# The second of every two gathered expert rows summed on VectorE instead of TensorE, in the PEER stage of a decoder layer

## The reference, cut to what matters

```python
g = jax.nn.softmax(best_s, axis=-1)
a = jax.nn.gelu(jnp.einsum('nd,nhkd->nhk', hx, expert_u[eidx])) * g      # 128 numbers per token
return jnp.einsum('nhk,nhkd->nd', a, expert_v[eidx])                      # weighted sum of 128 rows of V
```

## Time and profile before

| | us |
|---|---|
| median of 3 runs (lowest, highest) | 4863.4 (4863.33, 4865.5) |
| the profiled execution | 4853.14 |
| its span, first to last instruction | 4851.3 |
| busy in it: TensorE, VectorE, ScalarE, GpSimd | 3906.1, 2540.8, 1380.6, 1277.3 |

### The profile page before, as it was taken

One profiled execution on the slowest core, in us unless ns is written; L12 is line 12 of the kernel. 1 busy time (PEld: TensorE's weight loads), 2 busy tenths in 40 slices (PEclk: granted clock), 3 DMA queues, 4 the chain that ended last, 5 costly groups with the idle time before them and its releaser, 6 DMA issues.

```text
span 4851.3 us, 41498 instructions
## 1 busy us (share of the span) xinstructions
PE 3906.1 (81%) x13477; PEld 2361.7 (49%) x13477; DVE 2540.8 (52%) x6112; ACT 1380.6 (28%) x4112; POOL 1277.3 (26%) x1078
## 2 busy tenths in 40 slices
PE   6788979999963999777998987777768777777786
PEld 5457366888853888643444442323223323232232
DVE  1564543433534112275867866557557465575574
ACT  1355432322321111212332332323223223222232
POOL 0000000001000000004444544444444445445443
PEclk8889979995985899888999999999999999999999
DMA  3000111303014111229999999999999999999998
GB/s 140 5 2 12 39 49 33 98 36 122 36 62 156 52 40 67 109 69 378 403 421 410 412 419 414 420 421 411 421 420 411 421 417 418 422 412 422 420 411 355
DMA packets 219012, 1235.30 MB, mean 255 GB/s; under 512 B 25226, under 2 KB 51242, under 8 KB 85426
## 3 DMA queue, kind: packets, MB, share of 16 engines
q0 software_dynamic: 154512, 1117.85, 56.0%
q1 hardware_dynamic: 62834, 112.83, 6.8%
q10 hardware_dynamic: 1456, 2.04, 0.1%
HBM read 1210.15 MB, written 22.48 MB: 254 GB/s over the span
## 4 chain that ended last, share of the span: by engine, by line
DMA 29%; PE 16%; DVE 8%; ACT 2%; POOL 2%; issue 2%; POOLq 0%; SPq 0%; DVEq 0%; ACTq 0%
DMA ff_rows<-in_uv,pk_expert 28%; PE banks L2018 12%; DVE ff_rows L1827 3%; PE banks L1981 2%; POOL ff_rows L1790 2%; ACT ff_diag L1898 1%; PE banks L1991 1%; DVE pk_cand L1646 1%; DVE pk_cand L1643 1%; DVE pk_axes L1648 1%; ACT ff_a L1891 1%; ACT ff_gelu L1886 0%; PE banks L1944 0%; DMA ff_rows<-in_uv,ff_pick_tail 0%; DVE topi L1738 0%
## 5 line engine op out<-in xcount | busy, mean ns | idle before, releaser
L2018 PE MATMUL banks<-ff_rows,ff_diag 128*128 128x512 f32 x4128 | 1940.7, 617 | 577.5 <-ACT ff_diag L1898 562.4
L1790 POOL DMA_INDIRECT ff_rows<-in_uv,pk_expert x1024 | 1234.1, 1205 | 2075.3 <-PE banks L2018 1208.4
L1827 DVE CUSTOM_DVE_ANT_0 ff_rows<-ff_rows,ff_h_row 128x1024 f32<-128x1024 f32 x1032 | 1251.7, 1224 | 970.5 <-DMA ff_rows<-in_uv,pk_expert 957.9
L2018 PEld LDWEIGHTS banks<-ff_rows,ff_diag 128*128 128x128 f32 x4128 | 770.3, 194 | 1686.7 <-ACT ff_diag L1898 843.0
L1886 ACT ACTIVATE ff_gelu<-ff_dots 128x2 f32<-128x2 f32 x516 | 104.9, 203 | 1802.2 <-DVE ff_dots L1827 1801.9
L1898 ACT ACTIVATE ff_diag<-ident,ff_a 128x128 f32<-128x128 f32 x1024 | 355.0, 394 | 16.7
L173 PE MATMUL banks<-d_w_high,h_high 128*128 128x512 f32 (+1 forms) x648 | 274.2, 423 | 33.9 <-DVE d_w_low L180 33.6
L174 PE MATMUL banks<-d_w_low,h_high 128*128 128x512 f32 (+1 forms) x648 | 264.7, 408 | 0.0
L175 PE MATMUL banks<-d_w_high,h_low 128*128 128x512 f32 (+1 forms) x648 | 263.9, 407 | 0.0
L1891 ACT ACTIVATE ff_a<-ff_gelu,pk_gate 128x1 f32<-128x1 f32 x1024 | 245.7, 287 | 16.8
L1073 POOL DMA_DIRECT2D d_w<-in_w_dil x7 | 4.0, 575 | 884.9 <-POOLq L120 695.7
(11 more groups left out here) (343 smaller groups left out, 4704.6 us busy)
## 6 DMA issues: line engine op xcount, KB each, us to landing
d_w<-in_w_dil POOLq DMA_DIRECT2D x9, 2048.0 KB, 8.5
d_w<-in_w_ada POOLq DMA_DIRECT2D x32, 512.0 KB, 4.6
ff_w<-in_w_pq SPq DMA_DIRECT2D x32, 512.0 KB, 4.5
ff_rows<-in_uv,pk_expert POOLq DMA_INDIRECT x1024, 15.7
w_ada<-in_w_ada SPq DMA_DIRECT2D x16, 512.0 KB, 3.5
ds_kv<-in_state SPq DMA_DIRECT2D x8, 1024.0 KB, 8.1
mx_w<-in_w_gate SPq DMA_DIRECT2D x16, 512.0 KB, 5.6
o_group<-da_o SPq DMA_DIRECT2D x24, 260.0 KB
```

What stands on the lines that cost most here:

```text
L1790: pool.indirect_dma_start(out=rows[r][:, :], out_offset=None, in_=IN["uv"][:, :], in_offset=bass.IndirectOffsetOnAxis(ap=at, axis=0))\
L1827: ins = dve.tensor_tensor_reduce(rows[r][:, 0:D], rows[r][:, 0:D], h_row[t % 2][:], 1.0, 0.0, ALU.mult, ALU.add, dots[:, B % RB, j:j + 1])
L2018: ins = pe.matmul(A[0:n, half, :], diag[:, B % DB, j, 0:n], rows[r][:, D + half * 512:D + (half + 1) * 512], **ends)
```

## The change

In each batch the first pick is summed as before, by products on TensorE. The second is summed on VectorE by one scaled addition, acc = v * a + acc, over 128 x 1024 numbers in SBUF. The first batch of a tile sets acc by a scaled copy. There are two accumulators, taken in turn by tiles. `diag` holds one matrix for a batch instead of two. VectorE does the addition of batch B - 1 after the two dots of batch B (and ahead of whatever picking is placed there). GpSimd now waits for the addition too (`vsum`), before it reuses the buffers. At the end of a tile `turn_out` waits for the additions, and makes each 128 x 128 block of T by two products into the same bank: `out` by the identity, and `acc` by the identity (for the sample tile by `ownerT`, which also sums the 16 partitions of a token).

```diff
-        diag = sb("diag", [P, DB, G, P])
+        diag = sb("diag", [P, DB, P])
+        acc = [sb(f"acc{i}", [P, D]) for i in range(2)]
@@ GpSimd, before the gathers of batch B
                     if B >= RB:
                         pool.wait_ge(s["sum"], B - RB + 1)
+                        pool.wait_ge(s["vsum"], B - RB + 1)
@@ VectorE
+                def sums(B):
+                    t, b = batches[B]
+                    r = B % RB * G + 1
+                    v, weight = rows[r][:, D:2 * D], a[:, B % RB, 1:2]
+                    dve.wait_ge(s["a"], B + 1)
+                    if b == 0:
+                        if t >= 2:
+                            dve.wait_ge(s["turn"], t - 1)
+                        ins = dve.tensor_scalar(acc[t % 2][:], v, weight, None, ALU.mult)
+                    else:
+                        dve.wait_ge(s["vsum"], B)
+                        ins = dve.scalar_tensor_tensor(out=acc[t % 2][:], in0=v, scalar=weight, in1=acc[t % 2][:], op0=ALU.mult,
+                                                       op1=ALU.add)
+                    ins.then_inc(s["vsum"], 1)
...
                     ins.then_inc(s["dot"], 1)
+                    if B:
+                        sums(B - 1)
...
+                sums(len(batches) - 1)
                 add_out(LAST - 1)
@@ ScalarE
-                    for j in range(G):
-                        ins = act.activation(diag[:, B % DB, j, 0:width], base[:, 0:width], ACT.Copy,
-                                             scale=a[:, B % RB, j:j + 1])
-                    ins.then_inc(s["diag"], 1)
+                    act.activation(diag[:, B % DB, 0:width], base[:, 0:width], ACT.Copy, scale=a[:, B % RB, 0:1])\
+                       .then_inc(s["diag"], 1)
@@ TensorE, turn_out
+                    pe.wait_ge(s["vsum"], first[t + 1])
+                    turned = c.ident if t < LAST else ownerT
                     for m in range(KD):
-                        ins = pe.transpose(T[:, m // 4, (m % 4) * P:(m % 4) * P + n], out[0:n, m * P:(m + 1) * P],
-                                           c.ident[0:n, 0:n])
+                        at = T[:, m // 4, (m % 4) * P:(m % 4) * P + n]
+                        pe.matmul(at, out[0:n, m * P:(m + 1) * P], c.ident[0:n, 0:n], start=True, stop=False)
+                        ins = pe.matmul(at, acc[t % 2][:, m * P:(m + 1) * P], turned[:, 0:n], start=False, stop=True)
@@ TensorE, batch loop
-                    for j in range(G):
-                        r = B % RB * G + j
-                        ends = dict(start=(b == 0 and j == 0), stop=(B + 1 == first[t + 1] and j == G - 1))
-                        for half in range(2):
-                            ins = pe.matmul(A[0:n, half, :], diag[:, B % DB, j, 0:n],
-                                            rows[r][:, D + half * 512:D + (half + 1) * 512], **ends)
+                    r = B % RB * G
+                    for half in range(2):
+                        ins = pe.matmul(A[0:n, half, :], diag[:, B % DB, 0:n],
+                                        rows[r][:, D + half * 512:D + (half + 1) * 512], start=(b == 0),
+                                        stop=(B + 1 == first[t + 1]))
```

More of the change, by code:

```diff
@@ L1718, in stage_ffn @@
         s = {n: c.sem("ff_" + n) for n in ("keys_in q_mm q_copy sc_mm sc_copy top small_in x_in stored tail_out tail_in "
-                                           "ht htc h_mm h_copy dot gelu a diag sum out turn y").split()}
+                                           "ht htc h_mm h_copy dot gelu a diag sum vsum out turn y").split()}
         Q, S, A, T = c.psum[:, 0:2], c.psum[:, 2:4], c.psum[:, 4:6], c.psum[:, 6:8]
```

## The result

The changed kernel takes 4965.23 us (median of 3 runs, 4963.03 to 4968.35) where the kernel before takes 4863.4: a ratio of 1.0218, with a 95% interval of 1.0197 to 1.0239. It is 102 us slower; the forecast was 81 slower, 4944 in a range of 4880 to 5005. The profiled execution is the median run, with a span of 4963.4 us against 4851.3.

The account below looks back on a forecast made before the run. The prediction took the gathers in `stage_ffn` to bound the kernel at 421 GB/s. Its terms, 48 (six tiles) + 32 (first two) + 1 (end), gave +81 us on 4863.4: 4944 us, range 4880 to 5005.

Parts of the forecast that it names:

- The bound, and TensorE's relief: In `stage_ffn`, gathers bind at 421 GB/s; halving TensorE's products to 1.85 us a batch is worth nothing in undisturbed batches.
- The addition: VectorE's scaled addition of 128x1024, once a batch: 1.29 us, or 1.21 us with overlap, bounds 1.15 and 1.35.
- The delay, and the cover: Picking stretch, tiles three to eight: batch 32's release 16.2 us late, queue covers 6.5, loss 10.4 a tile; +48 us.
- the better case among its unknown costs: Gather queue able to shrink to the shortest landing seen, 5.6 us: 2.9 us less in each of eight tiles, -23.
- The 0.7 that the prediction had to add: Fifth tile before the change: the delay rule gave 2.7 us lost, the window 3.4; the difference was added to each loss.
- The first two tiles: `top16` also on VectorE there: release of batch 32 27.2 us late, 21.4 us lost a tile, +16 each, +32 us.
- The end: After the last batch, `turn_out` issues 16 products for 8 transposes, twice: +1 us (0 to +3).
- Backlog: VectorE's late work round the picking delays buffer release and gathers: +48 us for six tiles, +32 for the first two.
- Issue bound: Rival: with VectorE full, GpSimd's gather issue binds; 2.75 us a gather loses 7 us a tile, +58, 5002 us; chance 0.10.
- Clock: Rival: TensorE falls to 1.2 GHz, costing time in the first two tiles; 5069 us throughout, 4991 for half; chance 0.07.
- Double rate: Rival: the addition runs as fast as the scaled copy, cost 0.67 us; +23, 4887 us, or no change, 4864; chance 0.09.
- Faster: Rival: present losses come from TensorE, so halved products win up to 25 us; three quarters give 4845 us; chance 0.06.

Follow-up runs that it names:

- e1_relief: Changed kernel without the scaled additions on VectorE, the gathers' wait for them and the second product of each turn; 4846.4 us, 0.9968 of the kernel before.
- e6_half_add: Changed kernel with VectorE waits behind each `top16` part and `differences`, and the addition over 512 of 1024 columns; 4879.3 us, 1.0037 of the kernel before.
- e5_two_waits: Changed kernel with VectorE waiting for its own last instruction behind each `top16` part and behind `differences`; 4924.0 us, 1.0135 of the kernel before.
- e2_both: Changed kernel with the second pick's products made on TensorE as well, beside the additions (two diagonals, four products a batch); 4943.6 us, 1.0184 of the kernel before.
- e4_wait: Changed kernel with VectorE waiting for its own last instruction behind each `top16` part only; 4933.5 us, 1.0152 of the kernel before.
- e9_dot_wait: Changed kernel with VectorE waiting for the batch's own two dots ahead of each addition; 4940.5 us, 1.0185 of the kernel before.
- e3_order: Changed kernel with the six tiles of each `top16` part in reverse order, the 8-partition instruction first; 4944.7 us, 1.0181 of the kernel before.

## Why the prediction was right, and where it was off

**The bound, and TensorE's relief.** Right. The undisturbed window stays at 422 GB/s with VectorE 73.5% busy (forecast 421 and 71%), and the relief alone is worth 2.5 us of stage (e1_relief).

**The addition.** Right: 1280 ns in the median, forecast 1.29 us. In the row of 3777.66 to 3781.15 of the fifth tile dots and additions follow each other as the forecast had them:

```profile
3777.66 1.22 DVE L1844 CUSTOM_DVE_ANT_0 ff_rows<-ff_rows,ff_h_row 128x1024 f32<-128x1024 f32 x1
...
3778.81 1.28 DVE L1834 SCALAR_TENSOR_TENSOR ff_acc<-ff_rows,ff_a,ff_acc 128x1024 f32<-128x1024 f32 x1
3780.01 1.22 DVE L1844 CUSTOM_DVE_ANT_0 ff_rows<-ff_rows,ff_h_row 128x1024 f32<-128x1024 f32 x1
3781.15 1.22 DVE L1844 CUSTOM_DVE_ANT_0 ff_rows<-ff_rows,ff_h_row 128x1024 f32<-128x1024 f32 x1
```

The addition takes 3780.01 - 3778.81 = 1.20 us net; the forecast took 1.21.

**The delay, and the cover.** The delay was right, the cover was too small. GpSimd's timeline of the changed kernel in the fifth tile, the gathers of batch 20 and of batch 37 (which reuses the buffers of 32):

```profile
3679.43 1.48 POOL L1792 DMA_INDIRECT ff_rows<-in_uv,pk_expert  x1 [2.57 <-DVE ff_acc L1834]
...
3780.86 1.17 POOL L1792 DMA_INDIRECT ff_rows<-in_uv,pk_expert  x1 [8.60 <-DVE ff_acc L1834]
```

They are 101.4 us apart, undisturbed it would be 17 x 4.97 = 84.5: 16.9 us late, forecast 16.2. The tile lost 8.4, so the queue covered 8.5 of them. Its landings say the same: 14.2 us in an undisturbed window, down to 5.7 in this tile's picking stretch.

```profile
DMA to landing us min/median/max: 14.2/14.2/15.1
...
DMA to landing us min/median/max: 5.7/11.0/16.7
```

The prediction had 5.8 (15.0 - 8.5 - 0.7). It had named the better case among its unknown costs, a queue that shrinks to 5.6 us, worth 23 us less; this is what happened, with 5.7. Why did the sum not have it? It measured the old kernel's worst delay from batch 25. But batch 25 was late itself. Batch 20 of that tile was issued here:

```profile
3603.88 0.94 POOL L1790 DMA_INDIRECT ff_rows<-in_uv,pk_expert  x1 [3.11 <-PE banks L2018]
```

From it to batch 38 at 3705.03 it is 101.15 - 18 x 4.97 = 11.7 us late, and not 9.9 (which should read 10.0, as 74.60 - 64.6); with 3.6 lost, 8.1 were covered. Counted from batch 20 the four kernels agree: before 11.7 late, 3.6 lost; e6_half_add 10.9 and 3.8; changed 16.9 and 8.4; e5_two_waits 17.9 and 9.2. The cover is 7.1 to 8.7. The 0.7 that the prediction had to add should have been the hint: the rule did not close on the kernel before, and I patched it instead of asking from where I counted. In e5_two_waits, which has the backlog alone, tiles 3 to 8 lose 8.7 us each (forecast 10.4), 5.95 more than before (forecast 8.0): 36 us for six tiles where the forecast had 48.

**The first two tiles.** 20.9 us each in e5_two_waits, forecast 21.4; against 5.95 before it is +30 us, forecast +32. Two errors meet here: with a cover of 8.1 the forecast delay of 27.2 would have given 19.1. Where the other 1.8 came from no run says.

**The end.** Forecast +1 (0 to +3). From the last issue to the end it is 4963.4 - 4924.2 = 39.2 us, before 35.8: +3.4, just outside. Of it 0.9 is there in e1_relief already (36.7), so some 2.5 hang on the additions and on the products of `acc` in the last `turn_out`.

**The block.** This is the step that failed. The prediction had the issue of gathers as a bound of +8 us, and as a rival that made every gather of a full stretch slower, 2.75 us on the mean. The median did not rise (948 ns). What rose was the extreme: 28 issues of 4.7 to 12 us, 23 of them in the first two tiles, worth 36.5 us (36.3 by the stage). I had taken the longest issue of before, 3.53 us, for a harmless end of the range; it was the mark of this mechanism. VectorE's and GpSimd's timelines of before around it:

```profile
2391.18 3.53 POOL L1790 DMA_INDIRECT ff_rows<-in_uv,pk_expert  x1 [0.30 <-issue]
...
2391.35 0.27 DVE L1739 MATCH_REPLACE8 ff_sc_rest<-top,ff_sc 8x128 f32<-8x128 f32 x1
2391.54 1.20 DVE L1827 CUSTOM_DVE_ANT_0 ff_rows<-ff_rows,ff_h_row 128x1024 f32<-128x1024 f32 x1
...
2392.68 1.21 DVE L1827 CUSTOM_DVE_ANT_0 ff_rows<-ff_rows,ff_h_row 128x1024 f32<-128x1024 f32 x1
...
2393.83 1.24 DVE L1741 MAX8 top<-ff_sc_rest 128x8 f32<-128x128 f32 x6
```

The gather ends at 2394.71, 0.9 us after the second dot, whose row `top16` (L1741, one input) breaks off. Such a row was two dots long then; with the additions, and with VectorE further behind, it is nine instructions long. Rows of six dots alone can do it too: the 4.02 us of e1_relief, and three of 3.95, lie in such rows.

**The sum.** Backlog +65.5 (forecast +80), block +36.5 (0), in all +102.0 by the loss; the length of the stage says +103.7. Around it the end, +3.4 (forecast +1), and the start of the stage, 5.0 us later in this execution, which the change does not touch: 112.1 between the two spans. The median rose by 102 and not by 112, because the profiled execution of before lay 10 us under its median. That the forecast of 4944 came as near as 21 us is in part luck: one term was 15 us too large, another of 36 was missing, and the two errors go opposite ways.

**The rivals.** Issue bound: the typical 0.94 and 1.51 plus twice 0.3 make 3.05 us, and not the 3.7 of the prediction, so this rival was further off than it said; what came in its place is the block. Clock: its condition came true in part (0.74 to 0.81 in the loop), its price did not (e1_relief, e2_both). In the first two tiles TensorE, with two products a batch and the queries, is busy 71 and 75 of 120 us at 0.81 and 0.80, and VectorE, later than it, 118 and 111. Double rate: did not happen for two inputs (1280 ns), but the scaled copy of the first batch of a tile, L1831, does take 749 ns, as the earlier trace rows said for 1032 columns. Faster: fell with e1_relief, since TensorE's part in the losses of before was 2.5 us of stage and not three quarters of 25.

## What to carry to other kernels

A second engine's work is not free because that engine has idle time on the average. Sum its work from the last moment at which the queue was full to the release that comes latest, take off what the queue can give (here 7 to 9 us of a landing of 14 to 16; the rule must close on the kernel before without a correction), and the rest is lost; if the background work that makes the stretch can be spread out, the same addition costs little (here 9 us in place of 67). Look at the longest issue of a gather and not at its median, before more two-input work goes to VectorE.

## What the runs showed of the hardware

An indirect gather issued on GpSimd while VectorE goes through an unbroken row of instructions with two inputs in SBUF can be held to the end of the row, up to 11.97 us. Whether it is held depends on what stands ahead of the row. Where VectorE has just been held up by a semaphore, for itself too, no issue was held over 4 us, as here in the fifth tile, in the middle of dots and additions:

```profile
3754.23 1.22 DVE L1844 CUSTOM_DVE_ANT_0 ff_rows<-ff_rows,ff_h_row 128x1024 f32<-128x1024 f32 x1
...
3757.73 1.22 DVE L1844 CUSTOM_DVE_ANT_0 ff_rows<-ff_rows,ff_h_row 128x1024 f32<-128x1024 f32 x1
3758.58 1.17 POOL L1792 DMA_INDIRECT ff_rows<-in_uv,pk_expert  x1 [10.21 <-DVE ff_acc L1834]
...
3760.02 1.30 DVE L1834 SCALAR_TENSOR_TENSOR ff_acc<-ff_rows,ff_a,ff_acc 128x1024 f32<-128x1024 f32 x1
3760.06 0.94 POOL L1792 DMA_INDIRECT ff_rows<-in_uv,pk_expert  x1 [0.30 <-issue]
```

Its addition takes 1.30 us where those of the held rows take 1.27, as if here VectorE gave way for a moment and there it did not. That one wait behind `top16`, behind `differences`, or within the row ends the long issues is shown (e4_wait, e5_two_waits, e9_dot_wait). Why a wait that is over before the row begins should change how the row behaves is open. A missing wait alone does not make the block: behind `differences` on 128 partitions the issue takes 1.58 us, behind `differences` on 8 partitions 10.90. Behind `top16` the size of the last instruction does not decide (e3_order). What the two cases have in common is not known.
